# Gated delta layer: one projection piece moved from the fifth solve step to the end of the block

## The reference, cut to what matters

```python
qkv = silu(causal_conv(qkv, conv_w)); q, k, v = split(qkv)
q = l2norm(heads(q)) * DK_A ** -0.5;  k = l2norm(heads(k))
beta = sigmoid(b);  gc = cumsum(g);  decay = exp(gc_i - gc_j)      # causal
lmat = where(strict, (k*beta) @ k.T * decay, 0)
tmat = inverse(lmat + eye)                                         # lower triangular
u = tmat @ (v*beta);  w = tmat @ (k*beta*exp(gc));  attn = q @ k.T * decay
for each chunk:                                                    # scan over chunks
    v_new = u - w @ S
    o = (q*exp(gc)) @ S + attn @ v_new
    S = S * glast + kg.T @ v_new
o = rmsnorm(o, g_norm) * silu(z)
```

## Time and profile before

| | us |
|---|---|
| median of 3 runs | 4340.06 (4339.73 to 4340.58) |
| the profiled execution, its own time | 4340.02 |
| its span, first to last instruction | 4337.8 |
| the delta layer in it, from its first projection piece to its last matmul | about 2024 to 3006 |

### The profile page before, as it was taken

One profiled execution on the slowest core, in us unless ns is written; L12 is line 12 of the kernel. 1 busy time (PEld: TensorE's weight loads), 2 busy tenths in 40 slices (PEclk: granted clock), 3 DMA queues, 4 the chain that ended last, 5 costly groups with the idle time before them and its releaser, 6 DMA issues. The chain is left out here.

```text
span 4337.8 us, 60108 instructions
## 1 busy us (share of the span) xinstructions
PE 3924.5 (90%) x23467; PEld 2732.3 (63%) x23467; DVE 2621.4 (60%) x4970; ACT 1367.4 (32%) x2908; POOL 892.1 (21%) x544
## 2 busy tenths in 40 slices
PE   8999999997999999987999999987999998998877
PEld 5555555554666556655888888876656565565544
DVE  5656656564665666653565566662256676778875
ACT  1222222221111111111333333331244454565552
POOL 1334433442222221221222222220000000000000
PEclk9999999998999999998999999996999999999998
DMA  7343333434433343324000000022110100000000
GB/s 263 110 142 136 122 135 128 142 107 156 138 126 129 121 140 130 131 88 135 23 21 26 23 26 26 16 69 74 30 35 18 35 18 27 25 18 18 18 13 17
DMA packets 196048, 342.14 MB, mean 79 GB/s; under 512 B 19173, under 2 KB 99386, under 8 KB 195642
## 3 DMA queue, kind: packets, MB, share of 16 engines
q1 hardware_dynamic: 195770, 338.26, 22.4%
HBM read 298.90 MB, written 39.33 MB: 78 GB/s over the span
## 5 line engine op out<-in xcount | busy, mean ns | idle before, releaser
L245 PE MATMUL e_ps<-arena 128*128 128x386 f32 (+1 forms) x1960 | 658.4, 488 | 5.5 <-DVE arena L295 2.9
L245 PE MATMUL o_ps<-arena 128*128 128x320 f32 x1624 | 488.1, 455 | 80.0 <-DVE o_hh L314 40.7
L245 PEld LDWEIGHTS e_ps<-arena 128*128 128x128 f32 x1960 | 364.6, 191 | 247.2 <-issue 21.0
L245 PEld LDWEIGHTS o_ps<-arena 128*128 128x128 f32 x1624 | 317.4, 201 | 215.4 <-issue 29.6
L1603 PE MATMUL d_ps<-hT_in,arena 128*128 128x128 f32 x3072 | 393.3, 283 | 13.4 <-ACT hT_in L1789 11.4
L1603 PEld LDWEIGHTS d_ps<-hT_in,arena 128*128 128x128 f32 x3072 | 360.5, 193 | 29.0 <-ACT hT_in L1789 12.6
L2393 PE MATMUL s_ps<-hT_in,arena 128*128 128x128 f32 x2160 | 257.4, 279 | 6.7 <-PEq L67 6.7
L2393 PEld LDWEIGHTS s_ps<-hT_in,arena 128*128 128x128 f32 x2160 | 253.7, 196 | 10.1 <-issue 9.1
L2517 PE MATMUL s_ps<-arena 128*128 128x512 f32 x512 | 228.3, 600 | 0.0
L1149 PE MATMUL o_ps<-o_w_out,o_gt 128*128 128x512 f32 x512 | 226.1, 600 | 0.0
L638 PE MATMUL e_ps<-e_w_out,e_gt 128*128 128x512 f32 x512 | 222.3, 592 | 0.0
(11 more groups left out here) (491 smaller groups left out, 6858.9 us busy)
## 6 DMA issues: line engine op xcount, KB each, us to landing
arena<-l_w_in SPq DMA_DIRECT2D x48, 1024.0 KB, 7.8
arena<-l_w_in SPq DMA_DIRECT2D x32, 1040.0 KB, 8.4
xb<-x SPq DMA_DIRECT2D x64, 512.0 KB, 5.0
arena<-l_w_in SPq DMA_DIRECT2D x16, 1544.0 KB, 9.2
arena<-l_w_in SPq DMA_DIRECT2D x16, 1280.0 KB, 7.4
arena<-l_w_in SPq DMA_DIRECT2D x32, 504.0 KB, 7.1
arena<-l_w_in SPq DMA_DIRECT2D x16, 768.0 KB, 6.0
o_scratch<-w_ada SPq DMA_DIRECT2D x16, 768.0 KB
```

What stands on the lines that cost most here:

```text
L245: m = pe.matmul(bank[(g + k) % 2][:, 0:self.n], rows[:, kk * P:(kk + 1) * P], cols[:, kk, :], start=(kk == 0 and k in (0, 1, 4)), stop=(kk ...
```

## The change

In the fifth solve step (s = 4) the second `fill()`, the one behind the matmuls of L1703, is left out. No piece is lost: the list holds one more from there on, and the last call of the body, `fill(17)`, takes all that is left.

```diff
@@ -1707,7 +1707,8 @@
                     m.then_inc(*RX_made.inc())
-                    fill()
+                    if s < 4:
+                        fill()
                     if not b.last:
```

## The result

| | before | changed |
|---|---|---|
| median of 4 runs, us | 4340.0 (4339.73 to 4340.58) | 4387.51 (4386.61 to 4389.87) |
| ratio to before, with its 95% interval | | 1.0110 (1.0093 to 1.0128) |
| span of the profiled execution | 4337.8 | 4384.7 |
| mean granted clock of the execution | 0.959 | 0.954 |

What follows compares the result with a forecast made beforehand. The prediction took TensorE to bound the delta layer. Per block -1.31 + 2.63 + 0.46 = +1.78 us, plus 1.50 per clock fall, times 14 gives 45.9 us: 4340.1 + 45.9 = 4386.0 us, range 4362 to 4400.

Steps and rivals of the forecast that it cites:

- part 1: Fifth solve step, L1703 to L1719: without the piece, 1.28 us with a bare wait for R, not 2.59; -1.31 a block.
- part 2: L1628 to L1648: ScalarE's copy, queued behind late piece 11, delays the squares; 8.82 us instead of 6.19, +2.63 a block.
- idle ahead of L1648: TensorE's new wait for VectorE's qn ahead of L1648, 2.4 us in each of blocks 0 to 13.
- part 3: L1648 to the next solve, L1687: two pieces cover the 1.03 us wait for T, 0.46 covers nothing; +0.46 a block.
- sum at a full clock: The three changed distances of a block added, clock staying at 1.00: +1.78 us per block, 24.9 us over 14.
- falls of the clock: Granted clock drops behind the new wait ahead of L1648, expected in each of 14 blocks, at 1.50 us per fall.
- Part 4: The clock: new idle time ahead of L1648 makes it fall in most blocks, priced at 1.50 us per fall.
- a rival for all blocks: Clock falls for longer behind the wait ahead of L1648: 3.0 us per block, 4407 us in total; chance 0.08.
- the likeliest case: Clock falls in most of blocks 0 to 13, priced as a fall in each: +45.9 us, 4386.0 us; chance 0.60.
- The rival "faster": ScalarE's copy not in the way, squares as early as before: -0.62 us per block, 4331.4 us; chance 0.04.
- The rival "the clock holds": Longer distances in blocks 0 to 13 as computed, but no clock fall: 4365.0 us; chance 0.24.
- The other signs: Expected in the profile: L1687's wait gone from blocks 1 to 14, about 0.6 us for R, clock about 0.97 over 2160 to 2900.

Runs made afterwards that it cites:

- part 1 or part 3 alone: Changed kernel with `fill(2)` for `fill()` in the first chunk's scan: 4345.82 us; kernel before with `fill(2)` for `fill(3)` ahead of L1648: 4339.44 us.

## Why the prediction was right

Forecast 4386.0 us, range 4362 to 4400; measured 4387.5.

| step | predicted, us a block | measured |
|---|---|---|
| part 1: L1703 to L1720 | 1.28 (-1.31) | 1.21 (-1.38) |
| part 2: L1628 to L1648 | 8.82 (+2.63) | 8.71 (+2.52) |
| idle ahead of L1648 | 2.4 | 2.33 |
| part 3: L1648 to L1687 | 6.42 (+0.46) | 6.67 (+0.71) |
| sum at a full clock | +1.78 | +1.85 |
| falls of the clock | 14 of 1.50 = 21.0 in all | 10, of 1.5 or 2.9 = 20.6 in all |

- *Part 1* held. The row of block 14 gave the distance with a bare wait to 0.07 us.
- *Part 2* held, and carries the case. The chain count from L1628 (copy 3.02, output square 3.51, squares 4.00) is in the trace 2454.83 - 2451.91 = 2.92, 3.41 and 3.89. The 0.1 us between them is piece 11's length, 1.95 instead of 2.05 us behind other full tiles. The chain behind the squares took from 3.89 to 8.71, 4.82 us, as in block 14 (5.95 - 1.13).
- *Part 3* was mis-sized by 0.25 us. Two pieces ahead of L1687 took 2467.29 - 2463.58 = 3.71 us, not 2 x 1.753 = 3.51. I had the 1.753 from three pieces between full tiles; between the key products and L1687, both on smaller tiles, the row of pieces costs 0.2 us more once. The 2.02 us of the one piece there showed it: 2.02 + 1.753 = 3.77 us is the length of the two in the trace. L1648 itself, the first work behind the wait, took 0.66 instead of 0.60.
- That the sum at a full clock came out within 0.07 us a block is in part luck: the misses of -0.07, -0.11 and +0.25 us cancel.
- *Part 4* had the right sum from two errors that cancelled. I expected a fall in every block at one price. There were 10, and four of them cost twice the price; twice the price I had put down as a rival for all blocks (4407 us), not as a part of the likeliest case, though the upper end of the range allowed for five long falls. The run with eight extra matmuls shows that the sum is the clock's, 20.6 us.
- The Trainium skill (TensorE: Matmul & The Clock Gate, section "A second HAM failure mode: psum-queue depth-cycling") has frequent short idle times between groups of matmuls make the clock swing. This case agrees for one length only: waits of 1.35 us and less did not do it (1.00 before, with part 1 or part 3 alone, and with the copy late), the one of 2.33 us with its short neighbours did.
- The rival "faster" named its own condition, the squares on time, and its price, -0.62 us a block. The run with the copy late made the condition true and gave -0.70. The rival "the clock holds" (4365.0 us) has its counterpart in the run with eight extra matmuls, 4366.7 us.
- The other signs: L1687's wait is left in 2 places, ahead of block 0 and of block 15 (1.03 and 2.98 us), and gone from blocks 1 to 14; that for R is 8.6 us over 16; the clock over 2160 to 2900 is 0.97, as said.

## What to carry to other kernels

When work moves later in one engine's order, look at what every other engine does with its result: an in-order engine that consumes it at a fixed place turns a late piece, urgent for nobody, into a delay of all that stands behind that consumer. Here one consumer moved along with its piece turned +1.1% into -0.2%, and cutting the pieces finer gave -0.5%. And price a new wait twice: its length, and what TensorE loses if the granted clock falls behind it, which here was four fifths as much again.

## What the runs showed of the hardware

- Filling a wait of TensorE with matmuls that nothing reads pays where the clock would fall: eight of them took 20.6 us off 14 blocks, and the filled last two blocks went from 95.6 or 104.6 to 84.4 us.
- The same two blocks, with nothing in them changed, took from 95.2 to 104.8 us in different kernels, and the time went with the clock: its mean over them was 0.72 where they took 95.2 or 95.6 us and 0.58 to 0.61 where they took 103 us and more. In 15 runs of the kernel before, on one chip, times from 4331.85 us (mean clock 0.961) to 4345.95 us (0.957) were seen. A difference of some us in the total can thus come from a stretch that the change does not touch, and the length of the steady blocks told more.
- A projection piece of 128x128 matmuls costs 1.98 us between matmuls of another shape and 1.79 us behind its like.
